# Hybrid decoder step on one core: C11 ahead of sums and splits, the gated lo part moved from GpSimd to VectorE, squares added earlier in even projection tiles

## The reference, cut to what matters

```python
def chunk_spatial_gate(h, w_in, ln_g, ln_b, w_s, b_s, w_out):
    z = gelu(h @ w_in); u, v = split(z, 2); v = layer_norm(v, ln_g, ln_b)
    mix = einsum('hij,ncjhd->ncihd', tril(w_s), v by chunks of 128) + b_s
    return (u * mix) @ w_out, v
def sq_relu_mlp(h, w_up, w_down):
    a = relu(h @ w_up); return (a * a) @ w_down
for layer in range(2):
    x = x + mixer(rms_norm(x, norm_mix_g[layer]))
    x = x + sq_relu_mlp(rms_norm(x, norm_ffn_g[layer]), w_ff_up[layer], w_ff_down[layer])
```

## Time and profile before

| | |
|---|---|
| median of three runs | 1243.57 us |
| the profiled execution | 1243.86 us, span 1242.2 us |
| busy: TensorE, VectorE, ScalarE, GpSimd | 97%, 69%, 49%, 5% |
| chain of work that ended last | TensorE 85%, VectorE 8%, ScalarE 3% |
| granted TensorE clock, mean | 0.989 of full speed |

### The profile page before, as it was taken

How to read it: one execution, slowest core, us unless ns; L and a number is a source line. 1 busy time by engine, 2 the same in 40 slices (tenths; PEclk the granted TensorE clock), 3 DMA queues, 4 the chain that set the end, 5 groups by cost and what they waited for, 6 DMA issues and landing times.

```text
span 1242.2 us, 23180 instructions
## 1 busy us (share of the span) xinstructions
PE 1199.2 (97%) x9394; PEld 1160.6 (93%) x9394; DVE 855.9 (69%) x1416; ACT 605.3 (49%) x1176; POOL 64.9 (5%) x111
## 2 busy tenths in 40 slices
PE   6999998999899999999999999989999999999998
PEld 5999886679899999999999999989999999999998
DVE  5798888766985684684686635668965855856852
ACT  5726654654564273373373424535752642642641
POOL 4010300000000000000000021030000000000000
PEclk9999998999999999999999999999999999999999
DMA  5322231253133143143132122222251241341412
GB/s 161 105 84 72 68 122 37 87 169 136 35 123 116 34 150 104 43 148 102 55 116 69 58 91 91 69 74 68 68 167 38 76 163 35 106 133 35 134 37 73
DMA packets 111777, 113.41 MB, mean 91 GB/s; under 512 B 6430, under 2 KB 105898, under 8 KB 111663
## 3 DMA queue, kind: packets, MB, share of 16 engines
q1 hardware_dynamic: 110111, 107.50, 26.8%
q0 software_dynamic: 1472, 4.41, 1.1%
q10 hardware_dynamic: 88, 0.02, 0.0%
HBM read 107.18 MB, written 5.16 MB: 90 GB/s over the span
## 4 chain that ended last, share of the span: by engine, by line
PE 85%; DVE 8%; ACT 3%; issue 1%; DMA 1%; POOL 1%; SPq 0%; ACTq 0%; DVEq 0%
PE ps L1270 31%; PE ps L1246 26%; PE ps L805 15%; PE ps L1044 5%; PE ps L957 1%; DMA w_raw<-in_w_in_ab 1%; PE ps L1165 1%; DVE w_lo L1843 1%; PE ps L987 1%; DVE c_f L1932 1%; DVE w_lo L2223 1%; PE ps L1004 1%; PE ps L969 1%; POOL A_lo L779 1%; DVE a_f L2460 1%
## 5 line engine op out<-in xcount | busy, mean ns | idle before, releaser
L1636 ACT ACTIVATE w_hi<-w_raw 128x512 fp32r<-128x512 f32 x320 | 197.5, 626 | 234.5 <-PE ps L1270 177.6
L2223 DVE TENSOR_TENSOR w_lo<-w_raw,w_hi 128x512 fp32r<-128x512 f32 x320 | 215.0, 686 | 11.9 <-ACT w_hi L1636 11.8
L1270 PE MATMUL ps<-A_hi,w_hi 128*128 128x272 f32 x1024 | 212.2, 288 | 0.0
L1270 PE MATMUL ps<-A_lo,w_hi 128*128 128x272 f32 x1024 | 212.0, 288 | 0.0
L1270 PE MATMUL ps<-A_hi,w_lo 128*128 128x272 f32 x1024 | 211.2, 288 | 0.0
L1270 PEld LDWEIGHTS ps<-A_hi,w_hi 128*128 128x128 f32 x1024 | 160.9, 188 | 0.1
L2382 DVE TENSOR_TENSOR t_f<-ps,r_all 128x544 f32<-128x544 f32 x64 | 46.4, 724 | 166.2 <-PE ps L1270 166.2
L1270 PEld LDWEIGHTS ps<-A_hi,w_lo 128*128 128x128 f32 x1024 | 160.9, 188 | 0.0
L1270 PEld LDWEIGHTS ps<-A_lo,w_hi 128*128 128x128 f32 x1024 | 159.9, 189 | 0.0
L1246 PE MATMUL ps<-B_lo,w_hi 128*128 128x272 f32 x512 | 147.7, 288 | 0.0
L1246 PE MATMUL ps<-B_hi,w_lo 128*128 128x272 f32 x512 | 147.6, 288 | 0.0
(11 more groups left out here) (337 smaller groups left out, 2446.6 us busy)
## 6 DMA issues: line engine op xcount, KB each, us to landing
w_raw<-in_w_ff_up SPq DMA_DIRECT2D x64, 512.0 KB, 4.7
w_raw<-in_w_ff_down SPq DMA_DIRECT2D x64, 512.0 KB, 5.2
w_raw<-in_w_in_ab SPq DMA_DIRECT2D x20, 512.0 KB, 4.7
w_raw<-in_w_in_c SPq DMA_DIRECT2D x16, 512.0 KB, 4.5
w_raw<-in_w_out_ab SPq DMA_DIRECT2D x8, 512.0 KB, 4.8
k_pg<-in_cache_k SPq DMA_DIRECT2D x16, 256.0 KB, 4.2
v_pg<-in_cache_v SPq DMA_DIRECT2D x16, 256.0 KB, 3.3
w_raw<-in_w_out_c SPq DMA_DIRECT2D x8, 512.0 KB, 4.4
```

Source lines behind the costliest of these rows:

```text
L1270: mm = pe.matmul(down_banks(u)[:, half, :], wt[:, k % KH, :], mv[:, k, half * HALF:(half + 1) * HALF], start=(k == 0 and at_ == 0), stop=( ...
L1636: act.activation(ring(w_hi, q), half_source(q), ACT.Copy).then_inc(fh_done, 1)
L2223: dve.tensor_tensor(ring(w_lo, q), half_source(q), ring(w_hi, q).bitcast(F32), ALU.subtract)\
```

## The change

Three edits, nearly all in VectorE's program. Nothing is computed differently.

1. In the first chunk of each layer C11 of pair 0 is read at p1.1 of VectorE's loop (in front of the split of the second p7) and C11 of pair 1 at p5.1 (in front of the split of the first p4). The s4 sum of pair 1 follows C11 of pair 0 instead of the split of p6.1, and the last square sum follows C11 of pair 1. Both C11 keep their waits, for p2 of their pair.
2. In even projection tiles of `to_ffn` the square sum of the tile before stands ahead of the wait for ScalarE's rounding instead of at the end of the tile's turn; in tile 6 the split of the fourth product (p5.1) stands there too, which was made in tile 5.
3. The subtraction for A_lo of the gated part moves from GpSimd to VectorE: that of head h - 1 stands between the bias additions and the multiplication of head h, the last one behind the loop. The multiplication's wait for GpSimd is gone.

```diff
@@ gpsimd
-            for k in range(KT):
-                pool.wait_ge(gh_done, k + 1)
-                pool.tensor_tensor(A_lo[:, k, :], a_f[:, k % 2, :], A_hi[:, k, :].bitcast(F32), ALU.subtract)\
-                    .then_inc(gl_done, 1)
@@ weights_lo
-                if name == "p6":
+                if name == "p6" and (c > 0 or u != 1):
                     weight_sum(layer, c, "s4", u)
@@ to_ffn
                     if j % 2 == 0:
+                        if j >= 2:
+                            square_sum(j - 1, index)
+                        if j == 6:
+                            weights_lo(q0 + 3)
                         dve.wait_ge(xh_done, KT * index + j + 1)
...
-                    if j >= 2:
+                    if j % 2 == 1 and j >= 3:
                         square_sum(j - 1, index)
                     if j < 4:
                         split_lo(j, n0 + j + 4)
                     else:
                         weights_lo(q0 + 2 * j - 8)
-                        if j < 7:
+                        if j in (4, 6):
                             weights_lo(q0 + 2 * j - 7)
@@ up_round
-                if (name == "p2" and u < 2) or (name == "p1" and u >= 2):
+                if c == 0 and (name, u) == ("p1", 1):
+                    part_11(layer, c, 0)
+                    weight_sum(layer, c, "s4", 1)
+                if c == 0 and (name, u) == ("p5", 1):
+                    part_11(layer, c, 1)
+                    square_sum(KT - 1, 2 * layer + 1)
+                if (name == "p2" and u < 2 and c > 0) or (name == "p1" and u >= 2):
                     part_11(layer, c, u)
@@ ffn_chunk
-                    if c == 0 and ORDER[u] == ("p1", 1):
-                        square_sum(KT - 1, 2 * layer + 1)
@@ gated part
+            def gated_lo(k):
+                dve.wait_ge(gh_done, k + 1)
+                dve.tensor_tensor(A_lo[:, k, :], a_f[:, k % 2, :], A_hi[:, k, :].bitcast(F32), ALU.subtract)\
+                    .then_inc(gl_done, 1)
+
             for h in range(H):
...
+                if h >= 1:
+                    gated_lo(h - 1)
                 dve.wait_ge(mix_ok, h + 1)
-                if h >= 2:
-                    dve.wait_ge(gl_done, h - 1)
                 dve.tensor_tensor(a_f[:, h % 2, :], u_f[:, h, :], v_f[:, h, :], ALU.mult).then_inc(gm_done, 1)
+            gated_lo(KT - 1)
```

## The result

The changed kernel takes 1229.81 us (median of 4 runs, 1227.67 to 1232.97), the kernel before 1242.49 beside it (4 runs, 1240.55 to 1243.95): ratio 0.990, 95% interval 0.9877 to 0.9923, so 9.6 to 15.3 us less. The forecast was 1232.5 in a range of 1229.5 to 1237.5.

What follows compares the result with a forecast made beforehand. TensorE, busy 1199.2 of 1242.2 us, bounds the kernel, so only its stops and low clock can yield gains. 4.24 + 1.51 + 1.86 + 2.1 + 1.62 = 11.33 us off 1243.86 gives 1232.5, range 1229.5 to 1237.5.

Steps and rivals of the forecast that it cites:

- What ends the stops at p6: TensorE's stops before p6 of pair 0, 4.24 and 1.86 us, end with C11, queued behind eight VectorE instructions.
- C11's new place: VectorE, first chunk: C11 of pair 0 comes 6.81 us after tile 7's addition instead of 9.23, so p6 follows without stopping.
- The margin of 0.3 us at the second p6: C11 of pair 1 done by 338.3 us, wanted at 338.6; if the slack goes, the second p6 waits.
- Even tiles: Layer 0 projection: four VectorE instructions leave the path by filling 1.23 us idle gaps, gaining 2.4 us.
- One sign of being wrong: Layer 0's even projection tiles still taking 5.5 us and more from addition to addition on VectorE.
- The stops and the clock behind the long one: At p6 of pair 0, removed stops gain 4.24 and 1.86 us, plus 1.51 of low clock in layer 0.
- The load of the fourth weight block: Feed-forward weights: landing 8.3 to 9.8 us behind p6's start, ScalarE 2 to 4 us late, no cost to TensorE.
- a wait for this buffer: A wait for w_raw in the first chunk, which would show the forecast wrong.
- Gated part: Gated lo part on VectorE: 0.72 us subtractions, a head every 2.08 us, TensorE's last part of tile 0 2.1 us earlier.
- The clock behind tile 0: After the last gated lo part: TensorE's clock no longer falls, gaining 1.62 us, with 0 as the other end.
- rival A: Gated product, tile 0: the clock falls all the same, giving 1234.1 us; chance 25%.
- The base: Starting time for the sum: the profiled execution's 1243.86 us; the three runs' median was 1243.57.

Runs made afterwards that it cites:

- C11 only: Kernel before with only C11, the s4 sum and the last square sum moved in VectorE's order; 1233.25 us (6 runs), ratio 0.9953.
- C11 too early: Changed kernel with both first-chunk C11 moved further ahead, to p1 of pair 0 in VectorE's loop; 1230.98 us (4 runs), ratio 0.9928.
- GpSimd beside: Changed kernel with unneeded GpSimd work beside the gated heads, additions for heads 0 to 3, memsets for heads 4 to 7; 1232.75 us (one run).
- gated part undone: Changed kernel with the gated subtractions given back to GpSimd; 1232.57 us (4 runs), ratio 0.9924.
- even tiles only: Kernel before with only the square sums and one split moved into the even projection tiles' gap; 1237.77 us (8 runs), ratio 0.9970.

## Why the prediction was right

By its own steps, in its order:

- **What ends the stops at p6.** C11, as argued from 341.19 against 341.30. Shown by C11 only: with its place alone changed, the stop shrank to 1.64 us, and C11's end moved with it.
- **C11's new place.** 6.81 us behind the addition of tile 7 in the forecast, 6.81 in the trace. Relative to p1.0 C11 of pair 0 starts at 7.77 us in layer 0 (forecast 7.6 to 7.7) and at 7.76 in layer 1 (7.75); that of pair 1 starts at 9.62 in layer 0 (9.64). The margin of 0.3 us at the second p6 held in both layers. C11 too early shows that it is a narrow one from the other side too.
- **Even tiles.** 2.4 us in the forecast; the addition of tile 7 comes 0.96 us behind p1.0 where it was 3.28, so 2.32. Tiles 2 and 4 keep a gap of 0.60 us before their rounding is there, since each got one square sum and no split. One sign of being wrong was set too low: I had named even tiles of 5.5 us and more from addition to addition in layer 0. Tile 6 still takes 6.23 (318.01 to 324.24), tiles 2 and 4 take 5.41 and 5.48. Before, the three took 6.70, 6.04 and 6.12; with tile 5, whose split moved to tile 6 (5.59 to 4.99), they give the 2.3 us. So that sign came although the step held.
- **The stops and the clock behind the long one.** 5.75 forecast, 5.84 measured. In layer 1, 1.86 and 1.95. The rest, 0.09 in each, is the restart: four products take 6.29 us behind a stop and 6.20 without one (15.30 − 9.10).
- **The load of the fourth weight block.** Forecast: issued 3.1 us behind p6, landing at 8.3 to 9.8, ScalarE 2 to 4 us late, TensorE not at all. The issue on SyncE and ScalarE's split of it, in the changed kernel:

```profile
335.47 0.92 SPq L613 DMA_DIRECT2D w_raw<-in_w_ff_up  x2
```

```profile
340.82 0.63 ACT L1631 ACTIVATE w_hi<-w_raw 128x512 fp32r<-128x512 f32 x1 [1.87 <-DMA w_raw<-in_w_ff_up]
```

  p6 starts at 332.38, so the issue is 3.1 and the landing 8.4 us behind it. ScalarE waited 1.87 us; TensorE did not stop. I had named a wait for this buffer as a sign of being wrong: it came, and its cover held.
- **Gated part.** A head in 2.08 us, subtractions at 0.72, the last lo part 2.16 us earlier (2.1). The stops of 1.3 "and up to as much" came as 1.06 and 0.79. GpSimd beside shows why 0.72 was the right end of 0.72 to 1.78.
- **The clock behind tile 0.** 1.62 forecast, 1.54 measured in the profiled pair. The value was right for this pair, the reason was not enough: I took the 1.86 us stop of layer 1, behind which nothing fell, as proof that such a stop does no harm. A stop of 1.88 with 1.07 and 0.28 ahead of it was followed by the low clock in five traces of seven. So the term is a chance, some 5/7 of 1.5 = 1.1 us a run as an estimate from these traces. The gated part undone, whose clock stayed up, is 2.2 us longer than the changed kernel in the rest, the gated gain without the clock. Behind the changed kernel's own stops, 0.79 and 1.06, the clock fell in none of the traces that have them or shorter ones, so rival A did not come as far as these show.
- **The base.** I summed from the profiled execution, 1243.86 us. It was on the late side, with the long stretch at the lower clock and the late load shown above: the median of the kernel before is 1242.49 beside the changed kernel and 1241.52 over 19 later runs. From 1242.49 the sum gives 1231.2; the measured median of 1229.81 is 1.4 below that, inside the spread of the four runs.

The parts overlap as the steps say: C11 only (clock fallen) saves 5.5 us of the rest and even tiles only 4.1; together, in the gated part undone, it is 9.2 with the clock up, thus 7.8 without that 1.4. That is 1.8 less than 5.5 + 4.1, mostly because each alone already saves the 1.51 us of low clock behind the long stop, which is gained once.

## What to carry to other kernels

A wait that a profile names for one instruction may hang on another in the same queue: look at what on the releasing engine ended within 0.1 us of the restart. An instruction with a wait of its own has a place in a queue that is right to within its slack on both sides; work out what it holds up as well as what holds it up. To weigh a change of 1%, compare stretches that begin just ahead of where the change first moves the engine that bounds: here the rest of the span repeats to 0.1 us, while the whole varies by more than 4.

## What the runs showed of the hardware

- The low clock behind the same three stops (1.07, 0.28, 1.88 us) came in five traces of seven; where it came, it cost 1.4 us (the rest of C11 only, 908.6 against 907.3).
- A GpSimd addition of two SBUF operands takes 1.34 us when it starts ahead of VectorE's subtraction, and the subtraction then takes 1.52. It takes 1.81 when the subtraction is already running, and VectorE's next operation, the multiplication, then takes 1.86. Beside a GpSimd write of 0.56 us the subtraction takes 0.73.
- The time ahead of layer 0's projection is not fixed: in three traces of one kernel p1.0 starts at 323.57, 325.21 and 327.96. In one of them the low clock lasts longer in a stretch of the attention, where TensorE waits for other engines: the stretch takes 17.68 us at a mean of 0.54 and 14.85 and 14.90 at 0.67 in the others. That is 2.8 of the 4.4 us; a weight load that lands later near 19 us makes most of the rest.
